# A hybrid attention, recurrence and mixture-of-experts layer on one core: projection chunks among the last heads, logit constants from columns, half-precision ranks, the first gather ahead of a slot's loads, and plain row reads at the end

## The chip, the core and the metric

The kernel runs on one core of one Trainium2 chip. The metric is the device time of one execution in microseconds. The core has a matmul engine (TensorE, in the profile PE, its weight loads PEld), a vector engine (VectorE, DVE), a scalar engine (ScalarE, ACT), GpSimd (POOL) and a synchronising engine (SyncE, SP), each with its own instruction stream. They meet through semaphores. Matmul results land in PSUM, eight banks of 512 float32 columns by 128 partitions. DMAs are issued from the streams of SP, ACT and POOL and share sixteen DMA engines.

## The reference

One layer of depth 1 over 640 rows of 1024 features: 512 latent tokens and 128 context tokens.

```python
h = modulate(rms_norm(x, lp['norm1']), sh1, sc1)
z = h @ lp['w_in']
q, k, v, xr, gb = jnp.split(z, ...)
attn = attend(q, k_all, v_all)                       # 8 heads of 64, 2 key/value heads
lru, finals = rg_lru(dw_conv(xr, ...), h0, ...)
x = x + g1 * (jnp.concatenate([attn, lru * jax.nn.gelu(gb)], axis=-1) @ lp['w_out'])
h2 = modulate(rms_norm(x, lp['norm2']), sh2, sc2)
x = x + g2 * moe(h2, ...)

# moe: top 1 of 4 groups, then top 2 of 8 experts in it; 32 experts of width 256
p_grp = softmax(x @ wg + bg); g_sel = argmax(p_grp)
fine_sel = (x @ we + be).reshape(-1, 4, 8)[g_sel]
top_v, top_i = lax.top_k(fine_sel, 2)
w_fine = softmax(top_v) * p_sel
y = sum over the two experts of w_fine * (silu(x @ w_gate) * (x @ w_up)) @ w_down
```

The outputs are both token groups, the new keys and values of the context rows, and the final recurrence states.

## The kernel before

The 640 rows are five tiles of 128 (`NT` = 5; the first four are latent, `LT` = 4). Every engine has one function with its program written out in order; nothing is scheduled by a tool.

**Attention.** The loop `for n in range(N + 7)` on TensorE runs over 40 pairs of tile and head. Turn `n` issues the scores of pair `n` (L1347), the five transpositions of the probabilities of pair `n - 3` (L1356, one for a context pair) and a part of the product with the values of four heads (L1374). VectorE takes the maximum (L938) and scales the probabilities (L944); ScalarE takes the exponential (L555) and copies the transposed probabilities out (L550). `mixT` counts finished tiles of attention output.

**Output projection.** After the loop TensorE transposes the final states (L1385) and 40 rows of modulation vectors into columns (L1388), and then issues `project(t, half)`: eight matmuls, one for each chunk `c` of 128 features, for each half of 512 columns of a tile (L1394). After tile 0 come the logit constants, `biases` (L1405): the modulation shift of each token group, spread by VectorE to 128 columns (L969), times the router weights, eight matmuls a group. From tile 1 on, the first chunks of a tile's projection, the transpositions of the previous tile (L1418), its logits (L1434) and its expert ranks (L1440, L1441) are interleaved.

**Routing.** VectorE picks group and experts of each row (L1021 to L1040). The ranks count, by matmuls with a triangle of ones (`tri`) and a matrix of ones in float32, how many earlier rows chose each expert. VectorE then turns ranks into steps and slots (L1091 to L1101), one half-precision product gives the token numbers of each step (L1467, `tid`), and two float32 products give the output rows and weights (L1472, L1477).

**Experts.** The experts are taken in 16 pairs, with 64 row slots for each expert of a pair; this run has 18 steps. Six experts' weights (3 MB each) fit into `ring`, so three pairs. SP loads experts 0 to 3 during and right after attention. The third slot, experts 4 and 5, is loaded when the last rows of `h2_rows` are in memory and the last logits are done. `refill(q, s)` loads pair `q` into slot `s` once the gate-up products of the slot's last step are done (`gu_mm`), and its down weights after `dn_mm`. POOL gathers the rows of a step from `h2_rows` (L691, L694) and scatters its results into `y_rows` (L710), which has 1280 rows: a row's first expert in the first 640, its second in the last 640. TensorE transposes the gathered rows (L1486), multiplies (L1502), transposes the activations (L1491) and multiplies again (L1516).

**Tail.** The last step's results are not scattered. SP reads the last 640 rows of `y_rows` into `yk` (L391), POOL adds the first 640 onto `X` by an accumulating DMA (L720), VectorE adds the two (`gathered`, L1183), and TensorE puts the last step's rows in place by a product with a 0/1 matrix (L1539), which VectorE adds (`finish`, L1189) before SP writes the tile (L394).

## Time and profile before

| | |
|---|---|
| median of 3 runs | 683.1 us (681.7 to 684.25) |
| profiled execution | 681.05 us, span 679.2 us |
| mean granted TensorE clock | 0.944 |
| PE busy | 601.5 us (89%) |
| DVE busy | 348.1 us (51%) |
| ACT busy | 176.5 us (26%) |
| POOL busy | 99.8 us (15%) |
| bytes moved | 173.02 MB, mean 255 GB/s |

A share of busy time is a mean over stages. Attention ends near 292 us, the projection and routing last to about 394 us, the expert steps from 407 to 654 us, and the tail takes the rest. The stage that a part of the change touches has to be read for itself, in a window or in the chain of waits.

### The profile page before, as it was taken

To read this page: it belongs to the slowest core of one execution; us is meant where nothing else is said; L and a number is where in the kernel's file an instruction comes from. 1 tells how busy PE (TensorE), PEld (TensorE's weight loads), DVE (VectorE), ACT (ScalarE), POOL (GpSimd) and SP (SyncE) were. 2 spreads that over 40 slices of the span, in tenths; PEclk is the share of its full clock that TensorE was granted. 3 is DMA by queue.
4 is the path that set the end of the run, shared out by engine and by line. 5 is a ranking of instruction groups with operands and counts; after the bars stand their busy time and mean duration, and the time that the engine had idled before them with its cause. 6 is when DMAs were issued, how large, how long until landed. Compare 5 with 4: busy or idle time off the path is not lost. (4 is left out here: it accounts for less than half of the span.)

```text
span 679.2 us, 9420 instructions
## 1 busy us (share of the span) xinstructions
PE 601.5 (89%) x3288; PEld 338.5 (50%) x3289; DVE 348.1 (51%) x774; ACT 176.5 (26%) x369; POOL 99.8 (15%) x136
## 2 busy tenths in 40 slices
PE   2778999899999899989999659999999998787856
PEld 0324454455656676636555455555555554444422
DVE  2455399764664988743666753334333342222226
ACT  4102387810123877711111000111101101000000
POOL 4000011121143000000000111222122221111120
PEclk9969899899999999989999858999999998888888
DMA  7999333360009729463001295999999999999587
GB/s 295 356 353 378 136 124 124 128 220 29 1 24 266 276 75 284 192 278 156 31 32 62 92 365 198 416 421 419 419 420 413 420 419 421 420 419 421 220 239 226
DMA packets 41539, 173.02 MB, mean 255 GB/s; under 512 B 10660, under 2 KB 15776, under 8 KB 26152
## 3 DMA queue, kind: packets, MB, share of 16 engines
q1 hardware_dynamic: 29984, 150.66, 56.6%
q0 software_dynamic: 7408, 18.20, 8.5%
q10 hardware_dynamic: 4120, 3.80, 1.7%
q8 instruction: 16, 0.26, 0.2%
q14 instruction: 11, 0.09, 0.0%
HBM read 161.74 MB, written 19.58 MB: 267 GB/s over the span
## 5 line engine op out<-in xcount | busy, mean ns | idle before, releaser
L1502 PE MATMUL ps<-expert_w,hT_mixT 128*64 128x256 f32 x1152 | 144.0, 409 | 16.1 <-DMA expert_w<-exp_w_up 15.2
L1502 PEld LDWEIGHTS ps<-expert_w,hT_mixT 128*64 128x64 f32 x1152 | 86.7, 142 | 78.2 <-issue 19.5
L1275 PE MATMUL ps<-hT_mixT,w 128*128 128x512 f32 (+1 forms) x256 | 76.0, 453 | 1.6 <-DVE hT_mixT L785 1.6
L1394 PE MATMUL ps<-w,hT_mixT 128*128 128x512 f32 x160 | 73.3, 606 | 0.0
L1516 PE MATMUL ps<-expert_w,w 128*64 128x512 f32 x288 | 65.8, 598 | 0.0
L618 ACT ACTIVATE w<-ps 128x128 f32<-128x128 f32 x36 | 10.0, 277 | 205.0 <-PE ps L1502 205.0
L1145 DVE SCALAR_TENSOR_TENSOR w<-w,ps 128x128 f32<-128x128 f32 x36 | 10.4, 288 | 101.7 <-ACT w L618 101.7
L1275 PEld LDWEIGHTS ps<-hT_mixT,w 128*128 128x128 f32 x256 | 40.5, 198 | 36.8 <-issue 35.1
L1287 PE MATMUL ps<-w_qkv,hT_mixT 128*128 128x512 f32 (+1 forms) x160 | 53.1, 488 | 0.0
L1163 DVE TENSOR_TENSOR w<-ps,w 128x1024 f32<-128x1024 f32 x18 | 22.0, 1225 | 56.8 <-PE ps L1516 56.6
L1394 PEld LDWEIGHTS ps<-w,hT_mixT 128*128 128x128 f32 x160 | 29.7, 194 | 32.0 <-issue 31.9
L1225 PE MATMUL ps<-w_mod_ring,silu_c 128*32 128x512 f32 x192 | 26.9, 663 | 21.0 <-DMA w_mod_ring<-w_mod 21.0
L1287 PEld LDWEIGHTS ps<-w_qkv,hT_mixT 128*128 128x128 f32 x160 | 29.8, 190 | 21.6 <-issue 19.7
L1516 PEld LDWEIGHTS ps<-expert_w,w 128*64 128x64 f32 x288 | 19.1, 136 | 33.0 <-issue 30.8
L938 DVE TENSOR_REDUCE softmax_stat<-ps 128x1 f32<-128x640 f32 (+1 forms) x40 | 28.6, 716 | 11.9 <-PE ps L1347 11.9
L1347 PE MATMUL ps<-k_stack,q_stack 128*128 128x320 f32 (+1 forms) x144 | 30.6, 331 | 3.2 <-ACT q_work L555 3.2
L710 POOL DMA_INDIRECT y_rows<-w,slot_row_now x17 | 23.9, 1408 | 57.7 <-DVE w L1163 53.5
L1347 PEld LDWEIGHTS ps<-k_stack,q_stack 128*128 128x128 f32 x144 | 21.3, 188 | 17.1 <-issue 11.9
L555 ACT ACTIVATE q_work<-ps,softmax_stat 128x640 f32<-128x640 f32 (+1 forms) x40 | 28.3, 707 | 3.9 <-DVE softmax_stat L939 3.5
L694 POOL DMA_INDIRECT w<-h_rows,slot_token_now x17 | 17.6, 1033 | 79.6 <-PE ps L1486 79.6
L550 ACT ACTIVATE w_qkv<-ps 128x640 f32<-128x640 f32 (+1 forms) x40 | 24.7, 618 | 14.2 <-PE ps L1356 13.8
L1356 PE MATMUL ps<-ident,q_work 128*128 128x128 f32 x168 | 25.3, 275 | 1.4 <-ACT w_qkv L550 1.4
(240 smaller groups left out, 742.4 us busy)
## 6 DMA issues: line engine op xcount, KB each, us to landing
expert_w<-exp_w_gate SPq DMA_DIRECT2D x32, 1024.0 KB, 16.1
expert_w<-exp_w_up SPq DMA_DIRECT2D x32, 1024.0 KB, 19.0
expert_w<-exp_w_down SPq DMA_DIRECT2D x32, 1024.0 KB, 22.1
w_mod_ring<-w_mod SPq DMA_DIRECT2D x24, 1024.0 KB, 6.3
y_rows<-zero_rows POOLq DMA_DIRECT2D x10, 512.0 KB, 9.2
w<-w_in SPq DMA_DIRECT2D x4, 1024.0 KB, 12.0
w<-w_out SPq DMA_DIRECT2D x4, 1024.0 KB, 11.8
w_qkv<-w_in SPq DMA_DIRECT2D x4, 768.0 KB, 14.2
```

The costliest lines, as they stand in the source:

```text
L550: act.activation(probT[:, m % HEADS, 0:k], wide[:, 4 * 512:4 * 512 + k], ACT.Copy).then_inc(S["pT_a"], 1)
L555: act.activation(probs(n), scores(n), ACT.Exp, scale=SCALE, bias=sm[:, 1, n:n + 1], accum_out=sm[:, 2, n:n + 1]).then_inc(S["prob"], 1)
L710: pool.indirect_dma_start(a["y_rows"], bass.IndirectOffsetOnAxis(pidc[:, 0:1], 0), y, None, bounds_check=TOP * TOK - 1, oob_is_err=False). ...
L938: step(dve.tensor_reduce(sm[:, 0, n:n + 1], scores(n), AXY, ALU.max))
L1225: ins = pe.matmul(ps[32 * q:32 * q + 32, 0, :], csil[:, c, :], wm[:, n % 2, q * 512:(q + 1) * 512], start=(c == 0), stop=(c == DC - 1))
L1275: ins = pe.matmul(ps[:, bank, 0:n], w1v[:, c, m * P:(m + 1) * P], HM[:, c, lo:lo + n], start=(c == 0), stop=(c == DC - 1))
L1287: ins = pe.matmul(ps[:, bank, 0:n], HM[:, c, t * P:(t + 1) * P], wqv[:, c, lo:lo + n], start=(c == 0), stop=(c == DC - 1))
L1347: ins = pe.matmul(ps[:, bank, 0:k], qs[:, h, t * P:(t + 1) * P], ks[:, g, s, lo:lo + k], start=(s == 0), stop=(s == 1))
L1356: ins = pe.transpose(ps[:, 4 + i // 4, (i % 4) * P:(i % 4 + 1) * P], prob[:, m % 3, i * P:(i + 1) * P], ident[:, :])
L1394: ins = pe.matmul(ps[:, 2 * (t % 2) + half, :], HM[:, c, t * P:(t + 1) * P], w1v[:, c, half * 512:(half + 1) * 512], start=(c == 0), stop= ...
L1502: ins = pe.matmul(ps[r, 2 + k, 0:2 * P].rearrange("p (k f) -> p k f", k=2), xT[:, c, r], w[:, :, c, k:FF:FC], start=(c == 0), stop=(c == D ...
L1516: ins = pe.matmul(ps[r, 5 + half, :], actT[:, c, r], ring[:, HOME[2 * s + i], lo:lo + 512], start=(c == 0), stop=(c == FC - 1))
```

## The change

- The chunks 0 to 2 of `project(0, 0)` are issued in turns `N + 1`, `N + 2` and `N + 3` of the attention loop.
- The transposition of the 40 modulation rows is issued in turn `N - 3`. In turn `N` eight matmuls with the router weights as the stationary operand and two shift columns as the moving one give the constants as a column of 36 for each token group. VectorE multiplies the identity by these columns (`spread`), and one matmul with ones gives all 128 partitions the 72 constants.
- VectorE's scale columns are made in its turn `N - 2`; the modulated router weights come before the two updates of `bc`, behind a wait for the last transposition.
- `pair`, `pre`, the triangle and the ones are float16 in the rank products; some scratch views have moved.
- SP waits for the first gather (`xg_in`) before it loads experts 4 and 5.
- SP reads both halves of `y_rows`; the first goes to `y0` in the free ring row 0. VectorE adds `X` to `yk` first (`with_second`), then `y0` (`with_first`). For tile 4 TensorE adds `y0` with a product by the identity.

```diff
+        count = sb("count_ones", [P, 2, P], F16)
...
+        spread = logit[:, :, :].rearrange("p t n -> p (t n)")[0:NG + NE, 0:2 * (NG + NE)]
...
-        pair = HM[:, 0:NT, 3 * NE:4 * NE]
+        pair = HM[:, 0:NT, 3 * NE:3 * NE + NE // 2].bitcast(F16)
...
-        pre = temp(1, 0, 2 * NE).rearrange("p (b n) -> p b n", b=2)
+        pre = temp(1, 0, NE).bitcast(F16).rearrange("p (b n) -> p b n", b=2)
...
+        y0 = ring[:, 0, 0:NT * D].rearrange("p (t n) -> p t n", t=NT)
...
             sp.wait_ge(S["lg_mm"], NT)
+            sp.wait_ge(S["xg_in"], 16)
             for j in (4, 5):
                 w_gate_up(sp, j, j)
...
+            for t in range(NT):
+                sp.dma_start(y0[:, t, :], a["y_rows"][t * P:(t + 1) * P, :]).then_inc(y0_in[t], 16)
...
             end = every_step_but_last(pool, step_of)
-            pool.wait_ge(S["y_out"], 16 * (end + 1))
-            pool.sem_inc(S["pool_turn"], 1)
-            for t in range(NT):
-                pool.dma_start(X[:, t, :], a["y_rows"][t * P:(t + 1) * P, :], accum_op=ALU.add).then_inc(xk_in[t], 16)
             pool.wait_ge(S["xg_in"], 16 * (end + 2))
...
+                if n == N - 2:
+                    dve.wait_ge(S["mod2_in"], 16 * 10)
+                    dve.wait_ge(S["route_in"], 16 * 6)
+                    step(dve.memset(ones, 1.0))
+                    dve.wait_ge(S["mrow_t"], 2)
+                    step(dve.tensor_copy(mcol2, ps[:, 5, 256:256 + 5 * DC]))
+                    dve.scalar_tensor_tensor(out=scalec, in0=scalec, scalar=1.0,
+                                             in1=mcol2[:, 4 * DC:5 * DC].unsqueeze(1).broadcast_to([P, 2, DC]),
+                                             op0=ALU.add, op1=ALU.mult).then_inc(S["prepared"], 1)
+                    dve.wait_ge(S["prepared"], 1)
+            dve.wait_ge(S["bias_mm"], 1)
+            for v in range(2):
+                ins = dve.tensor_scalar(spread[:, v * (NG + NE):(v + 1) * (NG + NE)], ident[0:NG + NE, 0:NG + NE],
+                                        ps[0:NG + NE, 5, 300 + v:301 + v], None, ALU.mult)
+            ins.then_inc(S["prepared"], 1)
+            dve.tensor_copy(count[:, 0, :], tri)
+            dve.memset(count[:, 1, :], 1.0)
+            dve.wait_ge(S["pT"], N)
+            for v in range(2):
+                dve.tensor_tensor(rwm[:, v, :, :], rw[:, :, :], scalec[:, v, :].unsqueeze(2).broadcast_to([P, DC, NG + NE]),
+                                  ALU.mult).then_inc(S["prepared"], 1)
             step(dve.scalar_tensor_tensor(out=bc[:, 0, 1, :], in0=bc[:, 0, 1, :], scalar=1.0, in1=shift2[:, :], op0=ALU.add, op1=ALU.mult))
             dve.scalar_tensor_tensor(out=bc[:, 1, 1, :], in0=bc[:, 1, 1, :], scalar=1.0, in1=shift2[:, :], op0=ALU.add, op1=ALU.mult)\
                .then_inc(S["bc_ok"], 1)
             dve.wait_ge(S["bc_ok"], 1)
-            def columns():
...
-                for v in range(2):
-                    dve.tensor_copy(shiftw[v], shiftc[:, v, :].unsqueeze(2).broadcast_to([P, DC, P])).then_inc(S["prepared"], 1)
...
             def biases():
-                dve.wait_ge(S["bias_mm"], 1)
-                dve.tensor_tensor(bias, ps[:, 6, 0:2 * (NG + NE)].rearrange("p (v n) -> p v n", v=2),
+                dve.wait_ge(S["bias_mm"], 2)
+                dve.tensor_tensor(bias, ps[:, 5, 320:320 + 2 * (NG + NE)].rearrange("p (v n) -> p v n", v=2),
                                   rb.unsqueeze(1).broadcast_to([P, 2, NG + NE]), ALU.add).then_inc(S["prepared"], 1)
...
-            def gathered(t):
+            def with_second(t):
                 dve.wait_ge(yk_in[t], 16)
-                dve.wait_ge(xk_in[t], 16)
                 step(dve.tensor_tensor(yk[:, t, :], yk[:, t, :], X[:, t, :], ALU.add))
+            def with_first(t):
+                dve.wait_ge(y0_in[t], 16)
+                step(dve.tensor_tensor(yk[:, t, :], yk[:, t, :], y0[:, t, :], ALU.add))
...
-            gathered(0)
-            gathered(1)
+            for t in range(NT - 2):
+                with_second(t)
             y_evict(end)
-            gathered(2)
+            for t in range(NT - 2, NT):
+                with_second(t)
+            with_first(0)
+            with_first(1)
             finish(0)
-            gathered(3)
+            with_first(2)
             finish(1)
-            gathered(4)
-            for t in range(2, NT):
-                finish(t)
+            with_first(3)
+            finish(2)
+            finish(3)
+            finish(4)
...
+                if n == N - 3:
+                    pe.wait_ge(S["mod2_in"], 16 * 10)
+                    pe.wait_ge(S["pT_a"], HEADS * LT)
+                    pe.transpose(ps[:, 5, 256:256 + 5 * DC], mrows[0:5 * DC, :], ident[0:5 * DC, 0:5 * DC]).then_inc(S["mrow_t"], 1)
+                if n == N:
+                    pe.wait_ge(S["route_in"], 16 * 6)
+                    pe.wait_ge(S["prepared"], 1)
+                    for c in range(DC):
+                        ins = pe.matmul(ps[0:NG + NE, 5, 300:302], rw[:, c, :], shiftc[:, :, c], start=(c == 0), stop=(c == DC - 1))
+                    ins.then_inc(S["bias_mm"], 1)
+                if n == N + 1:
+                    pe.wait_ge(S["wout_in"], 64)
+                    pe.wait_ge(S["mix_rec"], LC)
+                    pe.wait_ge(S["prob"], N - 1)
+                    project(0, 0, range(0, 1))
+                if n == N + 2:
+                    project(0, 0, range(1, 2))
+                if n == N + 3:
+                    project(0, 0, range(2, 3))
...
-            pe.wait_ge(S["mixT"], NT)
+            pe.wait_ge(S["mixT"], LT)
             pe.transpose(ps[0:UNITS, 7, 0:P], stcol[:, :], ident[:, :]).then_inc(S["st_t"], 1)
-            pe.wait_ge(S["mod2_in"], 16 * 10)
-            pe.transpose(ps[:, 5, 0:5 * DC], mrows[0:5 * DC, :], ident[0:5 * DC, 0:5 * DC]).then_inc(S["mrow_t"], 1)
...
-            def biases():
-                pe.wait_ge(S["route_in"], 16 * 6)
-                for v in range(2):
-                    pe.wait_ge(S["prepared"], v + 1)
-                    for c in range(DC):
-                        ins = pe.matmul(ps[:, 6, v * (NG + NE):(v + 1) * (NG + NE)], shiftw[v][:, c, :], rw[:, c, :],
-                                        start=(c == 0), stop=(c == DC - 1))
-                ins.then_inc(S["bias_mm"], 1)
...
-                pe.matmul(ps[:, 7, 64:64 + NE], ones, pre[:, t % 2, :], start=True, stop=False)
-                ins = pe.matmul(ps[:, 7, 64:64 + NE], tri, pair[:, t, :], start=False, stop=True)
+                pe.matmul(ps[:, 7, 64:64 + NE], count[:, 1, :], pre[:, t % 2, :], start=True, stop=False)
+                ins = pe.matmul(ps[:, 7, 64:64 + NE], count[:, 0, :], pair[:, t, :], start=False, stop=True)
                 if t == NT - 1:
-                    pe.matmul(ps[:, 7, 96:96 + NE], ones, pre[:, t % 2, :], start=True, stop=False)
-                    ins = pe.matmul(ps[:, 7, 96:96 + NE], ones, pair[:, t, :], start=False, stop=True)
+                    pe.matmul(ps[:, 7, 96:96 + NE], count[:, 1, :], pre[:, t % 2, :], start=True, stop=False)
+                    ins = pe.matmul(ps[:, 7, 96:96 + NE], count[:, 1, :], pair[:, t, :], start=False, stop=True)
                 ins.then_inc(S["rank_mm"], 1)
-            project(0, 0)
+            project(0, 0, range(3, DC))
+            pe.wait_ge(S["prepared"], 2)
+            pe.matmul(ps[:, 5, 320:320 + 2 * (NG + NE)], ones[0:NG + NE, :], spread, start=True, stop=True).then_inc(S["bias_mm"], 1)
             project(0, 1)
-            biases()
+            pe.wait_ge(S["mixT"], NT)
...
                     pe.wait_ge(S["fin"], t - 3)
+                    pe.wait_ge(y0_in[t], 16)
                 for half in range(2):
+                    if t >= 4:
+                        pe.matmul(ps[:, 2 * t % 8 + half, :], ident[:, :], y0[:, t, half * 512:(half + 1) * 512],
+                                  start=True, stop=False)
                     ins = pe.matmul(ps[:, 2 * t % 8 + half, :], chosen[:, t * P:(t + 1) * P],
-                                    y[:, half * 512:(half + 1) * 512], start=True, stop=True)
+                                    y[:, half * 512:(half + 1) * 512], start=(t < 4), stop=True)
```

TensorE, before, from the last transpositions of probabilities to the end of the constants (`q_work` holds probabilities, `w` under L1394 is the output projection's weights):

```order
L1356 MATMUL ps<-ident,q_work 128x128 [waits pT_a,prob_n] x3
L1374 MATMUL ps<-w_qkv,v_tok 64x256 [waits pT_a]
L1374 MATMUL ps<-w_qkv,v_tok 64x256
L1385 MATMUL ps<-ident,state_cols 8x128 [waits mixT,mix_rec,wout_in]
L1388 MATMUL ps<-ident,logits 128x40 [waits mod2_in]
L1394 MATMUL ps<-w,hT_mixT 128x512 x16
L1405 MATMUL ps<-router_w,x1T 128x36 [waits prepared,route_in]
L1405 MATMUL ps<-router_w,x1T 128x36 x7
L1405 MATMUL ps<-router_w,h_tok 128x36 [waits prepared]
L1405 MATMUL ps<-router_w,h_tok 128x36 x7
```

TensorE, the change, the same place:

```order
L1368 MATMUL ps<-par_cols,router_w 36x2 [waits prepared,route_in]
L1368 MATMUL ps<-par_cols,router_w 36x2 x7
L1397 MATMUL ps<-ident,q_work 128x128 [waits pT_a,prob_n]
L1350 MATMUL ps<-w,hT_mixT 128x512 [waits prob,mix_rec,wout_in]
L1397 MATMUL ps<-ident,q_work 128x128 [waits pT_a,prob_n]
L1350 MATMUL ps<-w,hT_mixT 128x512
L1397 MATMUL ps<-ident,q_work 128x128 [waits pT_a,prob_n]
L1350 MATMUL ps<-w,hT_mixT 128x512
L1415 MATMUL ps<-w_qkv,v_tok 64x256 [waits pT_a]
L1415 MATMUL ps<-w_qkv,v_tok 64x256
L1424 MATMUL ps<-ident,state_cols 8x128 [waits mixT]
L1350 MATMUL ps<-w,hT_mixT 128x512 x5
```

The constants' 16 matmuls behind tile 0 have become eight narrow ones ahead of the last three transpositions and one behind the first half of tile 0, and three chunks of the projection stand between those transpositions.

SP, before, the third slot's loads up to the first refill, with what each row waits for:

```order
L361 DMA w<-mod_rows 128x1024
L275 DMA expert_w<-exp_w_gate 128x2048 [waits h2_at1,lg_mm,h2_at0,h2]
L275 DMA expert_w<-exp_w_up 128x2048
...
L278 DMA expert_w<-exp_w_down 128x2048
L371 DMA hT_mixT<-k_tok 128x640 [waits route_ok,idx_mm]
L275 DMA expert_w<-exp_w_gate 128x2048 [waits gu_mm]
```

SP, the change, the same rows:

```order
L363 DMA w<-mod_rows 128x1024
L277 DMA expert_w<-exp_w_gate 128x2048 [waits lg_mm,h2_at1,xg_in,h2_at0,h2]
L277 DMA expert_w<-exp_w_up 128x2048
...
L280 DMA expert_w<-exp_w_down 128x2048
L374 DMA hT_mixT<-k_tok 128x640 [waits route_ok,idx_mm]
L277 DMA expert_w<-exp_w_gate 128x2048 [waits gu_mm]
```

The order is the same; the first of the six loads has one more wait, `xg_in`.

VectorE, before, the tail (`expert_w` is `yk`, `w<-ps` the last step's results):

```order
L1183 TENSOR_TENSOR expert_w<-expert_w,x_tok 128x1024 [waits xk_in0,yk_in0]
L1183 TENSOR_TENSOR expert_w<-expert_w,x_tok 128x1024 [waits xk_in1,yk_in1,v]
L1161 REGISTER_ALU [waits dn_mm,v]
L1163 TENSOR_TENSOR w<-ps,w 128x1024 [waits gsel,y_out]
L1183 TENSOR_TENSOR expert_w<-expert_w,x_tok 128x1024 [waits xk_in2,yk_in2]
L1189 TENSOR_TENSOR expert_w<-expert_w,ps 128x1024 [waits tail_mm,v]
L1183 TENSOR_TENSOR expert_w<-expert_w,x_tok 128x1024 [waits xk_in3,yk_in3]
L1189 TENSOR_TENSOR expert_w<-expert_w,ps 128x1024 [waits tail_mm,v]
L1183 TENSOR_TENSOR expert_w<-expert_w,x_tok 128x1024 [waits xk_in4,yk_in4]
L1189 TENSOR_TENSOR expert_w<-expert_w,ps 128x1024 [waits tail_mm,v]
L1189 TENSOR_TENSOR expert_w<-expert_w,ps 128x1024 [waits tail_mm] x2
```

VectorE, the change, the tail up to the fourth `finish`:

```order
L1187 TENSOR_TENSOR expert_w<-expert_w,x_tok 128x1024 [waits yk_in2,v]
L1166 REGISTER_ALU [waits dn_mm,v]
L1168 TENSOR_TENSOR w<-ps,w 128x1024 [waits gsel,y_out]
L1187 TENSOR_TENSOR expert_w<-expert_w,x_tok 128x1024 [waits yk_in3]
L1187 TENSOR_TENSOR expert_w<-expert_w,x_tok 128x1024 [waits yk_in4,v]
L1192 TENSOR_TENSOR expert_w<-expert_w 128x1024 [waits y0_in0,v]
L1192 TENSOR_TENSOR expert_w<-expert_w 128x1024 [waits y0_in1,v]
L1198 TENSOR_TENSOR expert_w<-expert_w,ps 128x1024 [waits tail_mm,v]
L1192 TENSOR_TENSOR expert_w<-expert_w 128x1024 [waits y0_in2]
L1198 TENSOR_TENSOR expert_w<-expert_w,ps 128x1024 [waits tail_mm,v]
L1192 TENSOR_TENSOR expert_w<-expert_w 128x1024 [waits y0_in3]
L1198 TENSOR_TENSOR expert_w<-expert_w,ps 128x1024 [waits tail_mm,v]
```

Three additions with `X` instead of two stand (the first is above these rows) ahead of the last step's results, none of them waits for a read of the first half, and four additions of `y0` come behind.

## Rows read from the trace of the kernel before

**Rows 1.** Windows, attention's end: us, busy of each engine, PEclk, DMA share, GB/s.
```profile
288.66:293.30 4.64, 2.14 (x11) 0.87 (x10) 3.30 (x6) 2.37 (x8) 0.00 (x0) 0.92 0.00 0
293.30:308.46 15.16, 15.16 (x34) 6.68 (x34) 4.48 (x9) 0.84 (x3) 0.19 (x1) 0.91 0.95 390
308.46:311.95 3.49, 3.49 (x34) 3.49 (x32) 2.08 (x3) 0.00 (x0) 0.00 (x0) 1.00 0.64 263
```

**Rows 2.** Timeline, PE, the last heads: start, us, engine, line, [idle before].
```profile
289.88 0.30 PE L1356 MATMUL ps<-ident,q_work 128*128 128x128 f32 x1 [0.89 <-ACT w_qkv L550]
```

**Rows 3.** The chain of waits: the first gather and the first gate-up product.
```profile
395.64 8.79 DMA w<-h_rows,slot_token
...
407.45 9.60 PE ps L1502 x64
```

**Rows 4.** Timeline, PE, from the last ranks to the routing products.
```profile
387.89 0.64 PE L1440 MATMUL ps<-hT_mixT,silu_c 128*128 128x32 f32 x2 [4.01 <-DVE hT_mixT L1040]
...
389.19 0.61 PE L1444 MATMUL ps<-hT_mixT,silu_c 128*128 128x32 f32 x2
393.94 0.50 PE L1467 MATMUL ps<-w,hT_mixT 128*128 128x37 f16 x10 [4.13 <-DVE w L1101]
...
398.70 4.46 PE L1477 MATMUL ps<-hT_mixT,w 128*128 128x37 f32 x20
```

**Rows 5.** Timeline, SP queue: the third slot's loads and the first refill.
```profile
391.19 0.33 SPq L275 DMA_DIRECT2D expert_w<-exp_w_gate  x1
...
417.09 0.33 SPq L275 DMA_DIRECT2D expert_w<-exp_w_gate  x1
```

**Rows 6.** Windows as in Rows 1: from the third slot's loads to the tail.
```profile
391.00:411.00 20.00, 12.61 (x66) 10.47 (x68) 10.26 (x33) 0.82 (x2) 2.65 (x2) 0.50 0.89 355
411.00:417.09 6.09, 6.09 (x51) 3.56 (x48) 0.64 (x2) 0.28 (x1) 0.18 (x1) 0.91 0.01 3
417.09:632.00 214.91, 202.39 (x1436) 110.38 (x1438) 72.77 (x128) 25.10 (x80) 45.12 (x64) 0.97 1.01 416
...
646.60:668.00 21.40, 12.13 (x57) 5.91 (x54) 6.69 (x9) 1.30 (x4) 4.79 (x5) 0.76 0.98 245
```

**Rows 7.** Timeline, PE, the last step and the tail.
```profile
640.43 9.07 PE L1502 MATMUL ps<-expert_w,hT_mixT 128*64 128x256 f32 x64 [2.69 <-DMA expert_w<-exp_w_up]
...
650.83 3.65 PE L1516 MATMUL ps<-expert_w,w 128*64 128x512 f32 x16
663.75 10.95 PE L1539 MATMUL ps<-w,hT_mixT 128*128 128x512 f32 x20 [9.27 <-DVE w L1163]
```

**Rows 8.** Timeline, DVE, the end.
```profile
650.43 0.55 DVE L1177 TENSOR_SCALAR hT_mixT<-hT_mixT 128x640 f32<-128x640 f32 x1
...
662.38 1.23 DVE L1163 TENSOR_TENSOR w<-ps,w 128x1024 f32<-128x1024 f32 x1 [0.20 <-DVE expert_w L1183]
```

**Rows 9.** DMA issues from 640 us to the end: KB each, us to landing.
```profile
expert_w<-y_rows SPq DMA_DIRECT2D x5, 512.0 KB, 8.6
x_tok<-y_rows POOLq DMA_DIRECT2D x5, 512.0 KB, 15.6
```

**Rows 10.** Timeline, SP queue, the end.
```profile
646.67 2.58 SPq L391 DMA_DIRECT2D expert_w<-y_rows  x5
...
675.99 0.33 SPq L394 DMA_DIRECT2D y_prompt<-expert_w  x1
```

**Rows 11.** Timeline, PE, the projection, logits and a rank in the middle.
```profile
316.34 3.60 PE L1394 MATMUL ps<-w,hT_mixT 128*128 128x512 f32 x8
319.77 1.87 PE L1434 MATMUL ps<-router_w_mod,x1T 128*128 128x36 f32 x16
...
325.85 0.30 PE L1440 MATMUL ps<-hT_mixT,silu_c 128*128 128x32 f32 x2
```

**Rows 12.** Timeline, POOL: after the second gather.
```profile
411.44 0.18 POOL L699 COPY slot_token_now<-slot_token 128x1 uint32 x1 [3.06 <-DMA w<-h_rows,slot_token]
```

**Rows 13.** DMA issues of the whole span: count, KB each, us to landing.
```profile
x_tok<-x_sample SPq DMA_DIRECT2D x4, 512.0 KB, 5.1
```

43 lines of the change are left out of this document (14 added, 29 removed).

## The prediction

> **What bounds the kernel now.** I read the granted clock and the 40 slices of the page first, then the chain of waits, then windows of each stage that the change touches, and last the timelines at their edges. 0.5% of the time, 3.4 us, is about what a measurement of this kernel can tell from no change.
>
> Four stages matter. At attention's end TensorE has run out of work: of the 4.64 us from 288.66 us it is busy 2.14, and the granted clock falls below full speed (0.92, then 0.91 in tile 0's projection) [rows 1]. It waits there for ScalarE's copies [rows 2]. From then to the last ranks TensorE is the bound.
>
> Then comes a stretch of latency. The first gather takes 8.79 us and lands at 404.43 us, and the first gate-up product ends at 417.05 us [rows 3]. The last routing product on TensorE ends at 403.16 us [rows 4], so only 1.3 us of that gather is exposed. The gather competes with the third slot's loads, issued from 391.19 us; the first refill follows at 417.09 us [rows 5].
>
> From there the DMA engines are the bound: share 1.01 at 416 GB/s for 215 us. Just ahead of it they are empty for 6.09 us (share 0.01), and 11% empty in the 20 us before [rows 6]. That hole is what the weight stream can win. The reader should see that the length of the expert stage is set by when this stream can run without a hole.
>
> The last gate-up product starts at 640.43 us, released by a weight load, and TensorE is done at 654.48 us. The last product waits until 663.75 us for the evicted results of the last step [rows 7]. VectorE had nothing else to do: it is free at 650.98 us [rows 8], but its first additions wait for POOL's accumulating reads, which take 15.6 us to land, against 8.6 us for SP's plain ones [rows 9] issued at 646.67 us [rows 10].
>
> **The change part by part.** Each time below is in the clock of the trace before.
>
> *Attention's end.* Three chunks go in between the last transpositions. A chunk is two of the eight instructions between 316.34 and 319.77 us, so 0.86 us [rows 11]; three are 2.57 us. The idle time there is 4.64 - 2.14 = 2.50 us [rows 1], its last part a wait for the context tile's copy, which tile 0's projection doesn't need. So all 2.5 us are filled. If TensorE doesn't idle, its clock stays full: sixteen chunks took 15.16 us [rows 1] where 16 x 0.86 = 13.7 are due, so 1.45 us more. The old constants go, 3.49 us [rows 1]. Added are eight narrow matmuls, 16 instructions. The trace has none with two columns: at the old constants' 3.49/32 = 0.11 us each they cost 1.75 us, at the half-precision products' 0.05 us each [rows 4] 0.8 us; I take 1.2. The product with ones is two instructions, 0.2 us. The transposition of the modulation rows only moves. Gain: 2.50 + 1.45 + 3.49 - 1.2 - 0.2 = 6.0 us. The bounds are 3.6 (dear narrow matmuls, the clock falls after all, and 0.4 us for VectorE's three extra instructions in its turn) and 6.5. Behind the new wait for `prepared` stand transpositions on which ScalarE and VectorE wait, but VectorE makes it two turns ahead. The `bc` updates end some 3 us later, which SP's loads of experts 2 and 3 wait for; nothing reads these weights before 407 us.
>
> *Ranks.* The last four rank products run from 387.89 to 389.80 us at half clock, eight instructions [rows 4]. In half precision there are four, at 0.05 us and some 0.25 us of latency: 0.45 us, a gain of 1.4 (bounds 0.95 by the instruction count alone, and 1.6). The four pairs in the middle [rows 11] are TensorE time in a stage bound by TensorE, 0.2 us each, 0.8 us in all (0.4 to 1.1). VectorE writes `pair` and `pre` with the same number of instructions.
>
> *Gather before loads.* At the ranks' end all is 6.0 + 0.8 + 1.4 = 8.2 us early. The gather without the loads beside it: the second one took 1.02 us of issue and 3.06 us after it [rows 12], with the DMA engines mostly idle. With the first one's longer issue I take 4.4 us, where 8.79 is the upper bound. It then lands at 400.0 us by the old clock, before the routing product's end, which becomes the late one; the row transposition gains 1.3 us. The first gate-up product ends 9.5 us early (5.5 to 10.5), and so do the refills' orders.
>
> The price is that the third slot's loads start at 400.1 - 8.2 = 391.9 us, 0.7 us later than now. They are six of 1 MB and the token numbers: 6.6 MB, 15.9 us at 416 GB/s. They end at 407.8 us, and the first refill is ordered at 417.09 - 9.5 = 407.6 us. So the stream has no hole any more, and step 2 needs those weights some 17 us later. Queued behind SP's new wait are only these loads, the token numbers and the refills. The second gather now runs against the loads; the transposition that needs it comes 10 us after its issue, against 8 to 9 us for a gather under load.
>
> What the stream gains is the empty time that goes. As a mean over engines this is 0.11 x 20 + 6.0 = 8.2 us, less 0.7 for the later start: 7.5 us. If one engine is always the last, it was busy until about 411 us, and the gain is 6.1 - 0.7 = 5.4 us. I take 6.7 us, between them; the end of the first gate-up product, 9.5 us, is the upper bound. TensorE's own steps start 9.5 us early, so they don't bind.
>
> For the lower of the two the Trainium skill has a reason, in "DMA: Bandwidth & Descriptors", section "Latency and other measured facts": two of the sixteen engines are usually slower than the rest. The views here don't show single engines, only a share that decays before 640 us. By that rule the stream's term would be 5.4 us and the sum 1.3 us less.
>
> *Tail.* VectorE is free at 650.98 us [rows 8]. Three additions with `X` at 1.23 us (the price of an addition over 1024 columns [rows 8]) bring it to 654.7, just after the last down product's end. Their reads, issued from 646.67 us [rows 10] and 0.5 MB each, should land from 650 us on. The eviction ends at 655.9 instead of 663.61 us. TensorE then needs 16 instructions for four tiles, 6.9 us at 0.43 us each [rows 11], and 3.4 us for tile 4 with the two added products, which VectorE's eleven remaining additions cover: 655.9 + 11 x 1.23 = 669.4 us. The last write takes from 675.99 to 679.2 us [rows 10], 3.2 us: the end is at 672.6, a gain of 6.6 us. Cover is lost if the first half's last read lands after some 663 us. Ten reads are 5.24 MB, 12.6 us at 416 GB/s, so about 661 us.
>
> *Sum.* 6.7 + 6.6 = 13.3 us. The profiled execution took 681.05 us and would take 667.75; the median shown is 2.05 us above it, so the forecast is 669.8 us. Its own range is 666 to 672.5, from the stream's 5.4 to 9.5 us and the tail's 5.5 to 7.
>
> **The rivals.**
>
> *The reads at the end are bound by the DMA engines, whoever issues them.* POOL's accumulates may have been slow because ten reads shared the engines: the window from 646.6 to 668 us has a DMA share of 0.98 at only 245 GB/s [rows 6]. Then the last of `y0` lands at 668 as now, tile 4 follows with 3.4 us, one addition and the write: 675.9, a gain of 3.3 in place of 6.6 us; 673.1 us in all. Against it speaks that this low rate came with the accumulates in the mix, while the weight loads' plain reads fill the same share with 416 GB/s. The Trainium skill says it in "DMA: Bandwidth & Descriptors", section "Issuing engines are not separate DMA queues": another issuing engine saves only the issue. Chance 13%.
>
> *The gather is slow by itself.* If it takes 8.8 us alone, the loads start at 396.3 us, 5.1 later than now, and of the stream's gain 1 to 3.1 us are left, say 2.0: 8.6 us in all, 674.5 us. The second gather's 4.1 us [rows 12] speak against it, though it may have had fewer rows. Chance 10%.
>
> *The stream's gain is lost inside it.* If the pace of the refills depends on TensorE's steps and not on the start, only the tail's 6.6 us remain: 676.5 us. Against it stands the share of 1.01 for all 215 us. Chance 7%.
>
> *Slower: the ten plain reads are served one after the other.* They share one queue. The first loads of the program, of the same size on the same queue, took 5.1 us each to land [rows 13]. At 5.1 us in series the last read lands at 646.67 - 6.7 + 51 = 691 us, and tile 4, its addition and the write end at 698.8: 19.6 us slower, 702.7 us. It is slower than before from 3.1 us a read on. Loads of 1 MB on that queue reach 416 GB/s together [rows 6], which speaks against it. Chance 4%.
>
> *The front doesn't shrink and the rest is eaten up*, so that no change shows: 3%.
>
> **How the numbers follow.** The forecast has 60%, the rivals 13, 10, 7, 4 and 3%, and 3% are for more than 17 us. The likeliest gives 669.8 us. The range from 665.5 to 675 us takes in the forecast's own range and the first two rivals; outside lie the other cases, 17%. Faster by over 0.5%: 60 + 13 + 10 + 7 + 3 = 93%; within 0.5%: 3%; slower: 4%.
>
> **What would show it.** In the changed profile, the idle entries of TensorE between the last transpositions of probabilities should be gone, its clock 1.00 through tile 0, and the first transposition of `x_tok` near 309.5 us instead of 315.5. The first gather should take some 4.4 us and end before the last routing product. The DMA share should be near 1 from about 392 us on without a hole, and the last gate-up product should start near 633.7 us. VectorE's eviction of the last step should follow its down product within 1.5 us. It is wrong if the gather keeps its 8 us, if the stream has a hole before the first refill, or if VectorE waits for `y0`.

## The result, and the profile after

The change takes 664.39 us (median of 4 runs, 660.76 to 665.64) against 682.44 us of the kernel before in the same comparison: a ratio of 0.972, 95% interval 0.968 to 0.977. That is 18.0 us by the medians; the two profiled executions are 681.05 and 665.64 us, 15.4 us apart (spans 679.2 and 663.8). The forecast was 669.8 us with a range from 665.5 to 675: right in direction, outside the range in size. In the experiments below one execution each of a_delay (677.23 us) and a_rank32 (707.91 us) ran at a lower granted clock than the others of its kernel; their medians here are of the other five.

Attention's end, TensorE, the change (columns as in [rows 2]):

```profile
289.15 0.69 PE L1368 MATMUL ps<-par_cols,router_w 128*36 128x2 f32 x16
289.77 0.33 PE L1397 MATMUL ps<-ident,q_work 128*128 128x128 f32 x1
289.94 1.02 PE L1350 MATMUL ps<-w,hT_mixT 128*128 128x512 f32 x2
...
298.01 0.44 PE L1465 MATMUL ps<-logits,silu_c 36*128 36x72 f32 x2
298.38 10.57 PE L1350 MATMUL ps<-w,hT_mixT 128*128 128x512 f32 x24
308.78 1.04 PE L1435 MATMUL ps<-ident,x_tok 128*128 128x128 f32 x8
```

No row has an idle entry, where the transposition in [rows 2] waited 0.89 us; and the first transposition of `x_tok` stands at 308.78 us (315.46 before). The windows say the same of the clock: 1.00 where [rows 1] has 0.92 and 0.91.

```profile
289.15:293.62 4.47, 4.47 (x32) 2.08 (x31) 3.15 (x13) 1.67 (x6) 0.00 (x0) 1.00 0.00 0
293.62:308.78 15.16, 15.16 (x37) 6.63 (x37) 6.31 (x10) 2.18 (x6) 0.19 (x1) 1.00 0.78 314
390.57:406.24 15.67, 14.68 (x90) 10.37 (x90) 4.27 (x8) 0.87 (x2) 1.19 (x2) 0.67 0.91 376
406.24:412.00 5.76, 5.76 (x36) 2.90 (x38) 1.91 (x4) 1.29 (x4) 1.21 (x2) 1.00 0.97 387
412.00:622.00 210.00, 198.04 (x1420) 108.41 (x1418) 71.97 (x128) 24.82 (x79) 43.90 (x62) 0.97 1.02 419
622.00:630.39 8.39, 3.32 (x16) 0.90 (x13) 2.79 (x4) 0.28 (x2) 2.47 (x3) 0.96 0.58 235
```

The last four rows answer to [rows 6]: the window ahead of the refills, which had a share of 0.01, is gone.

From the last ranks to the first gate-up product, TensorE, and the gather on POOL and the loads on SP (answering to [rows 3 to 5]; the last is the first refill):

```profile
379.96 0.21 PE L1457 MATMUL ps<-hT_mixT,count_ones 128*128 128x32 f16 x1 [4.01 <-DVE hT_mixT L1046]
389.62 4.46 PE L1496 MATMUL ps<-hT_mixT,w 128*128 128x37 f32 x20
393.88 1.95 PE L1505 MATMUL ps<-ident,w 128*128 128x128 f32 x8
396.82 9.38 PE L1521 MATMUL ps<-expert_w,hT_mixT 128*64 128x256 f32 x64 [0.99 <-DVE hT_mixT L1145]
```

```profile
386.56 1.65 POOL L699 DMA_INDIRECT w<-h_rows,slot_token  x1 [10.30 <-DVE slot_token L1114]
...
390.57 0.33 SPq L277 DMA_DIRECT2D expert_w<-exp_w_gate  x1
...
406.24 0.33 SPq L277 DMA_DIRECT2D expert_w<-exp_w_gate  x1
```

The gather takes 4.0 us (390.57 - 386.56) instead of 8.79, the row transposition no longer waits for it, and the refill is ordered 10.85 us earlier. The end, TensorE and then VectorE (answering to [rows 7, 8]):

```profile
630.39 10.30 PE L1521 MATMUL ps<-expert_w,hT_mixT 128*64 128x256 f32 x64 [5.07 <-DMA expert_w<-exp_w_up]
642.02 3.65 PE L1535 MATMUL ps<-expert_w,w 128*64 128x512 f32 x16
...
642.09 3.74 DVE L1187 TENSOR_TENSOR expert_w<-expert_w,x_tok 128x1024 f32<-128x1024 f32 x3
646.02 1.23 DVE L1168 TENSOR_TENSOR w<-ps,w 128x1024 f32<-128x1024 f32 x1 [0.20 <-DVE expert_w L1187]
```

```profile
expert_w<-y_rows SPq DMA_DIRECT2D x10, 512.0 KB, 7.9
```

VectorE evicts at 646.02 us, 0.35 us after the down product's end (642.02 + 3.65), and then works without a gap to 660.45. The last gate-up product starts 10.0 us earlier than in [rows 7]; from there to the span's end it is 33.4 us in place of 38.8.

### The profile page after: what moved, and what is told of

It reads as the page before. It is cut to its first block and busy times, and to the rows that moved or that the text cites. A ratio compares the mean times of both kernels' runs of the same rounds, so it can differ in the third digit from the quotient of the medians.

```text
span 663.8 us, 9384 instructions
## 1 busy us (share of the span) xinstructions
PE 593.3 (89%) x3266; PEld 331.4 (50%) x3267; DVE 351.9 (53%) x780; ACT 176.5 (27%) x369; POOL 95.0 (14%) x131
## 5 line engine op out<-in xcount | busy, mean ns | idle before, releaser
L1350 PE MATMUL ps<-w,hT_mixT 128*128 128x512 f32 x160 | 71.9, 597 | 0.0
```

The lines of the kernel that those rows point to most:

```text
L1350: ins = pe.matmul(ps[:, 2 * (t % 2) + half, :], HM[:, c, t * P:(t + 1) * P], w1v[:, c, half * 512:(half + 1) * 512], start=(c == 0), stop= ...
```

## The experiments

Executions differ in their first 216 us, whose program the change doesn't touch (last section), so places are compared inside one execution. Each place comes from one profile a kernel. G has to be read with the spread of the five kernels that are the same between T and the last gate-up product (the change, a_oldfront, a_oldtail, a_poolplain, a_tail2): 321.6 to 322.3. The medians of the kernels with the new parts come from 4 to 6 executions, which lie 2 to 9 us apart, so a difference of 2 to 3 us between two medians is not clear of noise. T is the first transposition of `x_tok`. The columns: the last scores of attention to T; T to SP's first load of the third slot (L) and to the first refill's order (B); T to the last gate-up product (G); from there to the span's end (E). All but the median and ratio are differences of timeline rows (E ends at the span's end).

| kernel | median, us | ratio to before (95%) | scores to T | L | B | G | E |
|---|---|---|---|---|---|---|---|
| before | | 1 | 27.89 | 75.73 | 101.63 | 324.97 | 38.77 |
| the change | 664.39 | 0.972 (0.968 to 0.977) | 20.62 | 81.79 | 97.46 | 321.61 | 33.41 |
| a_oldfront | 673.41 | 0.987 (0.982 to 0.992) | 27.87 | 81.88 | 97.90 | 321.70 | 32.19 |
| a_rank32 | 664.07 | 0.979 (0.974 to 0.985) | 20.63 | 84.20 | 99.33 | 324.68 | 32.76 |
| a_oldtail | 671.44 | 0.987 (0.983 to 0.991) | 20.63 | 82.61 | 98.46 | 322.34 | 38.61 |
| a_poolplain | 668.09 | 0.981 (0.977 to 0.985) | 20.63 | 82.21 | 98.45 | 322.24 | 35.05 |
| a_noahead | 666.82 | 0.978 (0.975 to 0.981) | 20.62 | 74.88 | 99.74 | 323.11 | 32.07 |
| b_ahead | 682.46 | 0.9995 (0.997 to 1.002) | 29.38 | 84.94 | 100.30 | 325.48 | 39.19 |
| a_delay | 667.66 | 0.981 (0.977 to 0.984) | 20.62 | 87.81 | 98.44 | 328.50 | 32.22 |
| a_split | 661.67 | 0.971 (0.968 to 0.975) | 20.62 | 74.93 | 98.45 | 322.06 | 32.22 |
| a_ktok | 664.31 | 0.973 (0.970 to 0.977) | 20.62 | 82.06 | 98.44 | 321.83 | 33.34 |
| a_warm | 666.76 | 0.978 (0.974 to 0.982) | 20.63 | 82.40 | 92.31 | 322.79 | 32.28 |
| a_warm_split | 664.12 | 0.975 (0.971 to 0.978) | 20.63 | 75.26 | 98.27 | 321.49 | 32.51 |
| a_stream | 662.13 | 0.969 (0.966 to 0.972) | 20.62 | 74.48 | 94.58 | 317.88 | 32.48 |
| a_tail2 | 665.07 | 0.976 (0.972 to 0.979) | 20.62 | 81.85 | 97.83 | 321.64 | 32.15 |
| a_all | 659.76 | 0.970 (0.965 to 0.975) | 20.62 | 74.64 | 92.34 | 317.36 | 31.83 |
| a_best | 662.40 | 0.970 (0.967 to 0.973) | 20.62 | 74.50 | 94.88 | 318.26 | 31.34 |

### What sets the end of the stream

**a_delay.** The loads wait for the first row transposition.

```diff
-            sp.wait_ge(S["xg_in"], 16)
+            sp.wait_ge(S["xt_mm"], 1)
```

> The change with the third slot's loads held back further: they wait for the end of the first row transposition (395.83 us) instead of for the gather (390.57), 5.3 us more. Nothing reads them before 418 us. Theory A (bytes): the loads end 5.3 us later, the first refill is ordered at 406.24 us as before but its bytes stand behind them, and the whole stream ends some 5 us later: 669.5 us. Theory B (order of the first refill): no change, 664.4 us within 0.7.

```profile
392.89 0.33 SPq L277 DMA_DIRECT2D expert_w<-exp_w_gate  x1
...
396.17 0.40 SPq L374 DMA_DIRECT2D hT_mixT<-k_tok  x1
403.52 0.33 SPq L277 DMA_DIRECT2D expert_w<-exp_w_gate  x1
```

```profile
633.58 9.07 PE L1521 MATMUL ps<-expert_w,hT_mixT 128*64 128x256 f32 x64 [2.78 <-DMA expert_w<-exp_w_up]
```

L grew by 6.0 us, the refill's order by 1.0, and G by 6.9. The order of the refill alone is not what counts. The median grew by 3.3 us; 1.2 of the 3.6 that are missing is in E, where the last gate-up product was shorter, the rest is not explained.

**a_noahead.** The wait is taken away.

> The change without its one new wait of SP: the third slot's loads no longer wait for the first gather. Theory A (the DMA engines are the bound from the third slot's loads on, and the end moves by the time in which the average engine is empty): the last rows of h2_rows are issued at 380.60 us and take 2.6 us to land, so the loads start at 383.2 us instead of 390.57 and are through by 399. The gather takes its 8.8 us of before, issued at 386.56, and lands at 395.4; the row transposition starts 1.5 us late (395.4 for 393.88), the first refill is ordered near 407.7 instead of 406.24. A hole opens between 399 and 408.7 us, but behind it the stream starts no later than in the change, where the slot's loads and the token numbers keep the engines busy until about 409.9. So 0 to 1.1 us faster than the change: 663.3 to 664.4 us. Theory B (the end keeps its distance to the order of the first refill): 1.5 us slower, 665.9 us. The prediction's own step (the wait brings the refill 1.3 us forward and costs nothing) agrees with B here.

```profile
392.45 1.95 PE L1504 MATMUL ps<-ident,w 128*128 128x128 f32 x8 [2.23 <-DMA w<-h_rows,slot_token]
```

The gather took 9.75 us beside the loads (382.70 to 392.45), and the row transposition waited 2.23 us for it. L fell by 6.9 us and gave nothing; B rose by 2.3 and G by 1.5 (the median by 2.4, within the noise). Here theory B is the better one. So either limit can bind.

**a_warm.** Eleven products without a reader keep TensorE busy in its waits.

```diff
+            def warm(n):
+                for i in range(n):
+                    pe.matmul(ps[:, 2, :], ident[:, :], X[:, 0, 0:512], start=True, stop=True)
...
             logits(NT - 1)
+            warm(4)
             rank(NT - 1)
+            warm(5)
             pe.wait_ge(S["slot"], TOP * NT + 1)
...
             ins.then_inc(S["idx_mm"], 1)
+            warm(2)
             pe.wait_ge(S["stepw"], 2)
```

> The change with eleven products of 128x512 whose result nobody reads, put into TensorE's waits around the last ranks (4 ahead of them, 5 behind, 2 ahead of the second routing product; 0.86 us each at full clock, in waits of 4.0, 4.6 and 2.1 us). In the change the granted clock is 0.50 from 378 to 400 us. If it stays at 1.00, the routing products end near 391 instead of 394.1 us, the row transposition and the first gate-up product take 1.0 and 7.4 instead of 1.95 and 9.4 us, and the first refill is ordered 5 to 6 us earlier, near 400.5 us. The slot's loads still start behind the gather at 390.6 us and end at 408. Theory C (the stream starts at the later of two things, the end of the slot's loads and the order of the first refill): hardly a gain, 663.4 to 664.4 us. Theory B (the end keeps its distance to the order of the first refill): 5.5 us faster, 658.9 us. If the clock doesn't stay up or the products delay the ranks: 664.4 us or up to 1 us more, with the refill's order where it was.

Window, the change and then a_warm:

```profile
378.00:400.00 22.00, 12.33 (x68) 10.39 (x70) 13.70 (x48) 0.82 (x2) 2.65 (x2) 0.50 0.46 182
```

```profile
378.00:400.00 22.00, 20.76 (x123) 12.36 (x124) 15.06 (x54) 1.10 (x3) 2.65 (x2) 0.96 0.41 155
```

SP and TensorE, a_warm:

```profile
401.84 0.33 SPq L277 DMA_DIRECT2D expert_w<-exp_w_gate  x1
...
632.32 9.07 PE L1528 MATMUL ps<-expert_w,hT_mixT 128*64 128x256 f32 x64 [2.98 <-DMA expert_w<-exp_w_up]
```

The clock held at 0.96, B fell by 5.2 us to 92.31, and G did not fall (322.79). This is the clearest of the runs: theory B wanted 5.5 us, theory C hardly anything. That the median is 2.4 us above the change's is not explained: G is 1.2 longer and E 1.1 shorter, and the intervals overlap.

**a_split and a_ktok** ease the loads' side alone.

```diff
+            w_gate_up(sp, 4, 4)
             sp.wait_ge(S["xg_in"], 16)
-            for j in (4, 5):
-                w_gate_up(sp, j, j)
-                w_down(sp, j, j)
+            w_down(sp, 4, 4)
+            w_gate_up(sp, 5, 5)
+            w_down(sp, 5, 5)
```

> The change with the gate and up weights of expert 4 (2 MB) loaded ahead of the first gather, the other four loads of the slot behind it as now. They start near 383.2 us, when h2_rows is in memory, and need 5 us; the DMA engines stand empty then. Theory A: the slot's loads end 5 us earlier, the token numbers as well, and the first refill's bytes start at its order, 406.24 us and one more for the latency, instead of about 409.9 us: up to 2.6 us faster than the change, 661.8 us. The gather may end up to 2 us later, which the routing products cover (it lands at 390.6, the transposition starts at 393.88). Theory B: no change, 664.4 us.

> The change with SP's load of the token numbers (0.33 MB, read only at the end) moved from behind the third slot's loads to behind the last refill. Theory A: the stream is shorter by its bytes, 0.33 MB at 419 GB/s or 0.8 us, and by up to 2 us if its small packets disturb the others: 662.4 to 663.6 us. Theory B: no change, 664.4 us. At the end the token numbers are wanted by VectorE near 641 us and should land near 630, so no loss there.

Neither moved G by more than 0.5 us. a_split's median is 2.7 us lower, a_ktok's is not, and the intervals overlap the change's. Inconclusive by the times. By the rule at the end of this section the two limits are 0.6 to 1.1 us apart in the change and the kernels like it, so that easing one wins at most that. The two together without the products of a_warm were not run; the rule gives them no more, since the refill's order would bind.

**a_warm_split, a_stream, a_all** move both limits.

> The same eleven products, and the gate and up weights of expert 4 loaded ahead of the first gather. Now both limits move: the slot's loads end some 5 us earlier, near 403 us and with the token numbers 404, the first refill is ordered near 400.5 us. Theory C: the end moves by 4 to 5 us, 659.9 us. Theory B: 5.5 us, 658.9 us, and the run with the products alone shows the same. Each alone would be worth nothing by C.

```profile
388.15 3.57 PE L1504 MATMUL ps<-hT_mixT,w 128*128 128x37 f32 x20
```

In its profile the clock fell to half before the last routing product ended (the row: 3.57 us, 2.42 in a_warm), and the first four unread products had run partly at half clock too (6.23 us, 5.21 in a_warm), which delayed the ranks: B stayed at 98.27, and G is 321.49. It tells nothing of both limits moved; it repeats a_split. a_stream adds the token numbers behind the last refill:

> The change with the eleven products in TensorE's waits, expert 4's gate and up weights ahead of the gather, and the token numbers behind the last refill; the tail and the last gate-up product are those of the change. Theory C (the stream starts at the later of the end of the slot's loads and the order of the first refill): both limits move, by 5 us and more if the clock stays full. From the first transposition of x_tok to the last gate-up product 317.4 us instead of 322.0, and the median 4.6 us below the change: 659.8 us. If the gain of the combined kernel came from its tail and its last product instead: 322 us between the two points and 664 us.

```profile
402.72 0.33 SPq L277 DMA_DIRECT2D expert_w<-exp_w_gate  x1
...
626.02 8.85 PE L1529 MATMUL ps<-expert_w,hT_mixT 128*64 128x256 f32 x64 [3.11 <-DMA expert_w<-exp_w_up]
```

B 94.58, G 317.88 (317.4 expected): 3.7 us less than the change, where either side alone had given nothing. Theory C holds in the profiles. The median gives less: 2.3 us in place of 4.6.

**b_ahead.** The kernel before with the wait alone.

```diff
             sp.wait_ge(S["lg_mm"], NT)
+            sp.wait_ge(S["xg_in"], 16)
             for j in (4, 5):
```

> The kernel before with SP's wait for the first gather alone. The gather lands some 4 us after its issue instead of 8.8, the row transposition starts at the end of the routing products, and the first refill is ordered some 1.3 to 2.5 us earlier, near 415 us. The slot's loads start at about 399.7 instead of 391.19 us and end near 416. Theory C: the later of the two counts, and they are nearly equal: with the loads and the token numbers through at 417 to 418 us the stream starts where it did before, to 1 us earlier: 681 to 682 us. Theory B (the refill's order alone): 1.3 to 2.5 us faster, 679.5 to 680.7 us. By the theory that empty time of the average engine counts, the delay of the loads costs what the hole gives back: 682 us.

0.9995 (0.997 to 1.002): no difference. The refill's order came 1.3 us earlier (B 100.30), the loads 9.2 us later (L 84.94), and G rose by 0.5.

The seventeen profiles together give one rule, with two numbers fitted to them: G is the later of L + 240.2 and B + 223.4 us. Where the loads bind (the change, a_oldfront, a_rank32, a_oldtail, a_poolplain, a_delay, a_warm, a_tail2, b_ahead), G - L is 239.7 to 240.7; where the refill's order binds (before, a_noahead, a_split, a_warm_split, a_stream, a_best), G - B is 223.2 to 223.6. In a_ktok both fit (239.8 and 223.4). The two limits lie far apart only in before and a_noahead (8 to 9 us, the order binds) and in a_delay and a_warm (6 to 7 us, the loads bind), and these four carry the rule; in all others they lie within 2.5 us of each other, in most within 1.1. In a_all the loads bind again: its four later loads start at 82.65 us with 5.0 us of loads behind them already, and there are 0.8 us of token numbers less, so 82.65 - 5.0 - 0.8 + 240.2 = 317.1, measured 317.36. The rule was read from these profiles and not put to a new one.

### What each part is worth

**a_oldfront.** Attention's end as before, all else as in the change.

> The change without its part at attention's end: no projection chunks among the last transpositions, the constants by sixteen products as before. Ranks, gather and tail are those of the change. The prediction's step prices this part at 6.0 us (3.6 to 6.5): 670.4 us. By the change's trace the first transposition of x_tok stands 6.7 us earlier than before although attention ran 0.4 us later: 7.1 us, 671.5 us. Rival: what the front wins is lost in the stream: 664.4 us.

The last scores stand 7.25 us further ahead of T (27.87 for 20.62), and G is unchanged, so nothing is lost in the stream. The median says 9.0; the 1.8 us more are within what executions of one kernel differ by.

**a_rank32.** `pair`, `pre`, `tri` and `ones` in float32 in the rank products, as before.

> The change with the rank products in float32 as before. The prediction's step prices them at 1.4 us at the end and 0.8 in the middle: 2.2 us, 666.6 us. In the change's trace the middle pair of rank products covers 0.05 us of TensorE where it took 0.36 before, so the middle is 1.2 us, and the last four end 0.3 us after their start instead of 1.9: 2.8 us in all, 667.2 us. Rival: the stream's end does not follow the start of the routing, no change: 664.4 us.

L and B are later by 2.4 and 1.9 us, G by 3.1. The times don't show it: the median is 0.3 us below the change's, the ratio 0.979 for 0.972 with intervals that overlap, and the five executions fall into 663.4 to 664.1 and 668.9 to 669.8 us.

**a_oldtail.** POOL's accumulates, one joint wait.

> The change with the tail of the kernel before: POOL's accumulating reads onto X, one joint wait for both reads, no added products on TensorE. The prediction's step prices the tail at 6.6 us (5.5 to 7): 671.0 us. Counted in the two traces from the start of the last gate-up product to the end of the span, the tail takes 38.8 us before and 33.4 after, so 5.4 us, in which the last gate-up product was 1.2 us longer in the change for its clock: by that 669.8 us. The rival that reads are bound by the DMA engines whoever issues them gives 3.3 us: 667.7 us.

```profile
647.22 1.23 DVE L1189 TENSOR_TENSOR expert_w<-expert_w,x_tok 128x1024 f32<-128x1024 f32 x1 [6.12 <-DMA x_tok<-y_rows]
651.01 1.23 DVE L1189 TENSOR_TENSOR expert_w<-expert_w,x_tok 128x1024 f32<-128x1024 f32 x1 [2.56 <-DMA x_tok<-y_rows]
652.43 1.22 DVE L1169 TENSOR_TENSOR w<-ps,w 128x1024 f32<-128x1024 f32 x1 [0.20 <-DVE expert_w L1189]
```

E is 38.61 us, with a last gate-up product of 8.93 us. With the new tail and one of 9.07 us it is 32.2 to 32.5 in a_delay, a_split, a_oldfront, a_warm and a_warm_split, 32.8 in a_rank32 and 33.3 in a_ktok. So the tail is worth 5.3 to 6.4 us. The median says 7.05.

**a_poolplain.** The first half read by POOL as plain copies.

```diff
+                pool.dma_start(y0[:, t, :], a["y_rows"][t * P:(t + 1) * P, :]).then_inc(y0_in[t], 16)
```

> The change with its five reads of the first half of y_rows issued by POOL as plain copies beside SP's five, instead of behind them. It tells apart what made the reads of before slow. If it was the accumulation, the ten plain reads still take 1.3 us each together, the second half's land at most every 2.6 us (in the change every 1.3, before every 3.8), and VectorE's first three additions, which stand ahead of the last step's eviction, wait up to 1.8 us: 664.4 to 666.2 us. If it was that two queues read at once, the second half's reads land every 3.8 us as before and the eviction is some 5 us late: 669 us.

```profile
expert_w<-y_rows SPq DMA_DIRECT2D x5, 512.0 KB, 7.3
expert_w<-y_rows POOLq DMA_DIRECT2D x5, 512.0 KB, 10.5
```

```profile
646.93 1.23 DVE L1189 TENSOR_TENSOR expert_w<-expert_w,x_tok 128x1024 f32<-128x1024 f32 x1 [1.53 <-DMA expert_w<-y_rows]
...
652.06 1.23 DVE L1189 TENSOR_TENSOR expert_w<-expert_w,x_tok 128x1024 f32<-128x1024 f32 x1 [1.36 <-DMA expert_w<-y_rows]
```

POOL's plain reads need 10.5 us where its accumulates need 15.2 (a_oldtail), so the accumulation is slow in itself. The rest is order: issued side by side the two halves share the engines, and VectorE waits 1.53 and 1.36 us for the half that it needs first. E is 35.05 us, 2.8 more than with the reads in a row and a last gate-up product of the same length (32.2), and the median is 3.7 us longer. That transfers of different issuers run on the same engines and interleave is what the Trainium skill states in "DMA: Bandwidth & Descriptors", section "Issuing engines are not separate DMA queues"; the trace agrees, with those two waits.

### A faster version

**a_tail2.** TensorE adds `X` of tile 1; two additions instead of three ahead of the eviction.

```diff
-            for t in range(NT - 2):
-                with_second(t)
+            with_second(0)
+            with_second(2)
             y_evict(end)
...
+            for half in range(2):
+                pe.matmul(ps[:, 2 + half, :], ident[:, :], X[:, 1, half * 512:(half + 1) * 512], start=True, stop=False)
             pe.wait_ge(S["chosen"], 1)
```

> The change with one of VectorE's fifteen additions of the tail moved to TensorE: the rows X of tile 1 are added by a product with the identity in TensorE's wait between the last down product and the evicted results (1.7 us), and two instead of three additions stand ahead of the eviction. In the change VectorE works without a gap from 642.09 to 660.45 us. If the tail is bound by VectorE, it ends one addition earlier, 1.2 us: 663.2 us. If it is bound by TensorE's products, no change: 664.4 us.

```profile
644.28 1.23 DVE L1168 TENSOR_TENSOR w<-ps,w 128x1024 f32<-128x1024 f32 x1 [1.39 <-PE ps L1536]
```

No gain (E 32.15, median 665.07 where 663.2 was expected): the addition saved became a wait of 1.39 us for the down product.

**a_all and a_best** put the pieces together; both add two products ahead of the last pair's gate-up product.

> All together as a candidate for a faster kernel: the eleven products, expert 4's gate and up weights ahead of the gather, the token numbers behind the last refill, one addition of the tail on TensorE, and two more products ahead of the last pair's gate-up product, which in the change runs 10.3 us instead of 7.4 for its clock. Theory C: 4.5 us from the stream, 0.8 from the token numbers, 1.2 from the tail, 0 to 1.6 from the last gate-up product: 656.3 to 657.9 us. By B the same within 1 us. If the products delay the real work where TensorE no longer waits, 1 to 2 us less gain.

> As the candidate before (eleven products, split loads, token numbers last, two products ahead of the last pair, rows X of tile 1 added on TensorE), with three of VectorE's additions ahead of the last eviction instead of two, because with two VectorE waited 1.4 us for the last down product. Theory C and a tail bound by VectorE: 0 to 1.2 us below the candidate's 659.8 us, so 658.6 to 659.8 us, and from the last gate-up product to the end 31 us. If the reads of y_rows bind the tail once the last gate-up product runs at full clock, it is no faster than the candidate.

```profile
623.17 7.47 PE L1530 MATMUL ps<-expert_w,hT_mixT 128*64 128x256 f32 x64
```

In a_all (the row) the last gate-up product runs at full clock. It brings little: the reads of `y_rows` then bind (VectorE waits 1.24 us for the first in a_all and 1.45 in a_best). Both medians miss what was expected, by 1.9 and 2.6 us. a_stream, a_all and a_best lie at ratios of 0.969 to 0.970, which can't be told apart; a_all has the lowest median, 659.76 us. By the medians they are 2.0 to 4.6 us below the change, by the ratios some 2 us (0.969 to 0.970 for 0.972), and their intervals overlap its own: that they are faster is likely by the profiles (G 3.4 to 4.3 us less) and not shown by the times.

## Why the prediction was wrong, point by point

- **The step that failed is "What the stream gains is the empty time that goes", taken as 6.7 us.** The last gate-up product moved by 10.0 us in the profiles, and by 10.2 with a G of 322.0, the mean of the change, a_oldfront, a_oldtail and a_poolplain (7.26 ahead of T, 2.97 behind it). That term is too small by 3.5 us (3.3 in the profile pair), and the measured gain is above its upper bound of 9.5 too, which was the forecast for the first refill's order: this came 10.85 us earlier. The 3.5 us have three parts.
  - The hole was priced too low, 1.6 us. This part rests on the rule above. With the prediction's own places (T at 309.5, loads at 391.9 us, so L 82.4) the rule above gives G 322.6 and a gain of 8.3 us. The middle value leaned on one engine that is always the last, which leaves 5.4 us; the mean over the engines, 7.5, was the nearer. But G - B is the same 223.3 us with a hole ahead of the refill (before) and nearly without one (a_stream): nothing of what the engines did ahead of the hole was carried behind it. And the hole ran longer than to the refill's order at 417.09 us: its first bytes move a microsecond later, which loads in flight hide. The windows of the kernel before:

```profile
417.00:418.00 1.00, 1.00 (x11) 0.99 (x9) 0.56 (x2) 0.53 (x2) 0.00 (x0) 1.00 0.00 0
418.00:419.00 1.00, 1.00 (x7) 0.46 (x7) 0.77 (x2) 0.77 (x2) 0.00 (x0) 1.00 0.81 164
```

  - Attention's end was priced at 6.0 us and is worth 7.26 (two profiles with the old form, fourteen with the new, within 0.03; b_ahead, at 29.38, had a granted clock of 0.52 for 7 us of it): 1.3 us. The narrow products took 0.69 us for 1.2, the product with ones 0.37 to 0.44 for 0.2, and the idle 2.5 us and the clock came as forecast. By the remainder some 0.9 to 1.0 us more came; no run takes it apart. It may be the products and transpositions that had stood alone and now run in a row: a lone transposition shows 0.30 us, eight in a row 1.04.
  - The loads start at L 81.8 instead of 82.4: the gather took 4.0 us for 4.4, and the ranks gave more. 0.6 us.
- **The slower engines.** The Trainium skill's rule that two of the engines are usually slower ("DMA: Bandwidth & Descriptors", section "Latency and other measured facts") was applied in the wrong place. What uneven engines would do shows at the end, where the share is 0.58 over the 8.4 us before the last gate-up product (0.49 before the change); after 16 us of loads little was carried. In the trace of the kernel before, the sixteen part-landings of each load after the first refill's order come within 1.1 us of each other, the last sixteen of the last pair's gate and up weights within 8.2 us. By that rule the term was 5.4 us; measured, it is 10.
- **Ranks and gather.** Forecast 2.2 + 1.3 = 3.5 us from T to the row transposition: measured 89.11 to 85.10, 4.0, and 3.2 to 4.0 by a_oldfront, a_oldtail, a_poolplain and a_tail2. Right. But "the price is that the loads start 0.7 us later" hid the main point: after the change the loads bind, not the refill's order. b_ahead shows the wait alone as worth nothing.
- **Tail.** Forecast 6.6 us, measured 5.4 in the profile pair, where the last gate-up product lost 1.2 us to its clock, and 5.3 to 6.4 by a_oldtail against the others. Right, its mechanism too: eviction 0.35 us behind the down product, no wait on `y0`. The longer last product stands nowhere in the prediction; by chance it hid 1.2 us of what the stream gained more.
- **From the profile to the median.** The prediction added 2.05 us because the median before lay that much above the profiled execution. The change's median lies 1.25 us below its own. So the offset is 3.3 us of the miss of 5.4, and it comes from outside the change. The other 2.1 are the profiled executions' own: 15.4 us gained for 13.3, which is 3.3 more in the stream and 1.2 less in the tail. The measured time lies 1.1 us below the range (whose own part, 666 to 672.5, is 666.6 to 672.2 by its terms); with either of the two put right, and the range moved by as much, it would have been inside.
- **The rivals.** Reads bound whoever issues them: no, a_poolplain's plain reads are quicker than accumulates. A gather slow by itself: no, 4.0 us. The stream's gain lost inside: no. Plain reads served one after another at 5.1 us: no, ten came with a median of 7.9 us to landing. The case of over 17 us, given 3%, is the one that the medians hit (18.0 us; the profiles, 15.4, do not).

## What to carry to other kernels

In this kernel a stream of transfers behind a hole had two limits, the end of what is queued ahead of it and the order of its first transfer. Where a kernel is built like this, work out both, and see which binds after the change, since the next gain needs both moved. Measure parts inside one execution, from one row to another, when executions differ by as much as the parts. The range should take in that difference between executions, not carry one of them over as an offset.
